# Feed-forward of a two-layer decoder: both parts of the tokens in one 512-column product, and the gate's K tiles ahead of the up's

## The reference

```
gate, up = split(h @ w_gu, (2816, 2816))
x = x + rms_norm((silu(gate) * up) @ w_down, g_post_ffn)      # the block

gate, up = split(conv3(h @ ffn_w_up) + conv_b, (2816, 2816))
x = x + (silu(gate) * up) @ ffn_w_down                        # layers 0 and 1
```

## Time and profile before

| What | Value |
|---|---|
| Time, median of 3 runs | 1380.72 us (1380.65 to 1381.92) |
| The profiled execution's own time | 1385.28 us |
| Its span in the trace | 1383.7 us |
| Mean granted TensorE clock | 0.98 |
| TensorE matmul busy | 1324.0 us, 96%, 8862 matmuls |
| DVE busy | 898.0 us, 65% |
| ACT busy | 685.7 us, 50% |
| POOL busy | 157.1 us, 11% |
| Read from HBM | 210.25 MB |

### The profile page before, as it was taken

How to read it: one execution, slowest core, us unless ns; L and a number is a source line. 1 busy time by engine, 2 the same in 40 slices (tenths; PEclk the granted TensorE clock), 3 DMA queues, 4 the chain that set the end, 5 groups by cost and what they waited for, 6 DMA issues and landing times.

```text
span 1383.7 us, 21580 instructions
## 1 busy us (share of the span) xinstructions
PE 1324.0 (96%) x8862; PEld 1190.6 (86%) x8862; DVE 898.0 (65%) x1325; ACT 685.7 (50%) x1007; POOL 157.1 (11%) x240
## 2 busy tenths in 40 slices
PE   6999999999999999999998999799999889899999
PEld 6987899878998898899997777699999767799998
DVE  5455378878646747644455676577776777676666
ACT  5345455635525546533344554554444675544443
POOL 8000030022000000300001131000000160000000
PEclk9999999999999999999999999999999999999999
DMA  8531355432645436566664622366666412366662
GB/s 279 189 121 63 124 177 177 147 108 92 227 154 183 181 95 197 153 183 184 186 188 130 213 92 82 86 183 183 183 183 202 162 32 77 91 185 186 187 186 95
DMA packets 207761, 212.69 MB, mean 154 GB/s; under 512 B 7473, under 2 KB 153859, under 8 KB 207664
## 3 DMA queue, kind: packets, MB, share of 16 engines
q1 hardware_dynamic: 204592, 206.25, 47.3%
q0 software_dynamic: 2480, 4.02, 0.8%
q10 hardware_dynamic: 592, 1.05, 0.2%
HBM read 210.25 MB, written 1.05 MB: 153 GB/s over the span
## 4 chain that ended last, share of the span: by engine, by line
PE 67%; DVE 6%; ACT 4%; issue 1%; POOL 0%; DVEq 0%; ACTq 0%
PE psum_a L515 8%; PE psum_a L516 8%; PE psum_a L517 8%; PE psum_b L515 8%; PE psum_b L517 8%; PE psum_b L516 8%; PE psum_c L516 4%; PE psum_c L515 4%; PE psum_c L517 4%; DVE w_lo L466 2%; ACT w_hi L456 1%; PE psum_c L2507 1%; PE psum_c L2477 1%; ACT junk_rows L683 1%; PE psum_c L2425 1%
## 5 line engine op out<-in xcount | busy, mean ns | idle before, releaser
L466 DVE TENSOR_TENSOR w_lo<-raw,w_hi 128x2048 fp32r<-128x2048 f32 (+4 forms) x221 | 423.0, 1947 | 72.7 <-ACT w_hi L456 71.7
L456 ACT ACTIVATE w_hi<-raw 128x2048 fp32r<-128x2048 f32 (+3 forms) x231 | 369.3, 1631 | 30.1 <-PE psum_b L517 16.3
L515 PE MATMUL psum_a<-x_hi,w_hi 128*128 128x256 f32 x752 | 216.2, 287 | 2.2 <-DVE w_lo L505 2.1
L515 PE MATMUL psum_b<-x_hi,w_hi 128*128 128x256 f32 x752 | 214.0, 285 | 0.8 <-issue 0.8
L516 PE MATMUL psum_a<-x_lo,w_hi 128*128 128x256 f32 x752 | 214.4, 285 | 0.0
L517 PE MATMUL psum_a<-x_hi,w_lo 128*128 128x256 f32 x752 | 214.2, 285 | 0.0
L516 PE MATMUL psum_b<-x_lo,w_hi 128*128 128x256 f32 x752 | 213.3, 284 | 0.0
L517 PE MATMUL psum_b<-x_hi,w_lo 128*128 128x256 f32 x752 | 213.2, 284 | 0.0
L515 PEld LDWEIGHTS psum_a<-x_hi,w_hi 128*128 128x128 f32 x752 | 146.1, 194 | 4.2 <-DVE w_lo L505 2.8
L516 PEld LDWEIGHTS psum_a<-x_lo,w_hi 128*128 128x128 f32 x752 | 146.0, 194 | 1.2
L515 PEld LDWEIGHTS psum_b<-x_hi,w_hi 128*128 128x128 f32 x752 | 144.8, 193 | 2.4 <-issue 0.9
(11 more groups left out here) (504 smaller groups left out, 2490.2 us busy)
## 6 DMA issues: line engine op xcount, KB each, us to landing
raw<-in_ffn_w_up_dram SPq DMA_DIRECT2D x88, 512.0 KB, 5.1
raw<-in_w_in_dram SPq DMA_DIRECT2D x40, 1024.0 KB, 5.6
raw<-in_w_gu_dram SPq DMA_DIRECT2D x44, 512.0 KB, 5.1
raw<-in_ffn_w_down_dram SPq DMA_DIRECT2D x44, 512.0 KB, 3.6
raw<-in_w_down_dram SPq DMA_DIRECT2D x22, 512.0 KB, 5.7
raw<-in_w_br_ssm_dram SPq DMA_DIRECT2D x8, 1024.0 KB, 5.0
raw<-in_w_xkv_dram SPq DMA_DIRECT2D x8, 1024.0 KB, 5.9
raw<-in_w_out_dram SPq DMA_DIRECT2D x8, 1024.0 KB, 5.1
```

Source lines behind the costliest of these rows:

```text
L456: act.activation(k.w_hi[:, s, 0:size], k.raw[:, s, 0:size], ACT.Copy).then_inc(*k.rounded.at(*key))
L466: dve.tensor_tensor(k.w_lo[:, s, 0:size], k.raw[:, s, 0:size], k.w_hi[:, s, 0:size].bitcast(F32), ALU.subtract).then_inc(*k.split.at(*key))
L515: pe.matmul(out_ap, l[0], r[0], start=start, stop=False, skip_group_check=True)
```

## The change

X becomes one tensor `X_both` of [128, 2 parts, 8 K tiles, 256 tokens]. `pe_gate_up` now issues, for each K tile and half, one matmul of w_hi with both parts of X (512 columns, in two chunks of 256) and one of w_lo with x_hi (256 columns). Each half has a bank of its own: columns 0 to 255 get w_hi x_hi and w_lo x_hi, columns 256 to 511 w_hi x_lo. Gate's eight K tiles come first, then up's; only block 0, which waits for X's K tiles one by one, keeps both halves inside the K loop. A signal `ffn_gate` tells that the gate's bank is made.

ACT copies the second half of each bank to SBUF (`both`), DVE adds the first half of the bank to it, and the taps, silu and product then read SBUF. Between them `dve_hidden` does the block's down piece in two halves (`dve_split_part`, the renamed `dve_split_third`), and DVE does the gate-and-up piece of h + 2 behind the hidden. `act_ffn` rounds two pieces ahead of every hidden but the first, so that its last one, behind the hidden of block 21, is now ahead of it. The memory keys are turned behind block 5's gate and up, into psum_a, and block 6 waits for their copy.

```diff
+        self.X_both = self.sb("x", [P, 2, KD, SEQ], F32R)
+        self.X = [self.X_both[:, part, :, :] for part in range(2)]
...
 def pe_gate_up(k, tag, h, after=None):
+    pe, ps, key = k.nc.tensor, ffn_ps(k, h), (tag, "gu", h)
     if h >= 2:
-        pe.wait_ge(*(k.ffn_h if tag == "ffn" else k.ffn_free).by(tag, h - 2))
-    for kt in range(KD):
-        if after:
+        pe.wait_ge(*k.ffn_both.by(tag, h - 2, 1))
+    for kt, j in [(kt, j) for kt in range(KD) for j in range(2)] if after else [(kt, j) for j in range(2) for kt in range(KD)]:
+        if after and j == 0:
             pe.wait_ge(*k.lo_made.by(after, kt))
-        for j in range(2):
-            mm = three(k, ps[:, j * SEQ:(j + 1) * SEQ], [x[:, kt, j * P:(j + 1) * P] for x in w], [x[:, kt, :] for x in k.X],
-                       kt == 0 and j == 0, kt == KD - 1)
+        hi, lo = (x[:, kt, j * P:(j + 1) * P] for x in w)
+        pe.matmul(ps[:, 512 * j:512 * j + 512].rearrange("p (n t) -> p n t", n=2), hi, k.X_both[:, :, kt, :], start=kt == 0,
+                  stop=False, skip_group_check=True)
+        mm = pe.matmul(ps[:, 512 * j:512 * j + SEQ], lo, k.X[0][:, kt, :], start=False, stop=kt == KD - 1, skip_group_check=True)
+        if (kt, j) == (KD - 1, 0):
+            mm.then_inc(*k.ffn_gate.at(tag, h))
...
 def act_hidden(k, tag, h, layer):
+    for j in range(2):
+        act.wait_ge(*(k.used.by(tag, "gu", h) if j else k.ffn_gate.by(tag, h)))
+        act.activation(k.both[:, u, j, :], ps[:, 512 * j + SEQ:512 * j + 512], ACT.Copy).then_inc(*k.ffn_copy.at(tag, h, j))
...
 def dve_hidden(k, tag, h, layer):
+    halves = h != FT - 3
+    for j in range(2):
+        dve.wait_ge(*k.ffn_copy.by(tag, h, j))
+        dve.tensor_tensor(k.both[:, u, j, :], ps[:, 512 * j:512 * j + SEQ], k.both[:, u, j, :], ALU.add).then_inc(*k.ffn_both.at(tag, h, j))
+    if halves:
+        dve_split_part(k, 0, 2)
...
+    if halves:
+        dve_split_part(k, 1, 2)
...
 def act_ffn(k, tag, layer):
     act_ffn_clear(k, tag)
-    act_split(k, 1)
-    act_hidden(k, tag, 0, layer)
-    for h in range(1, FT):
+    for h in range(FT):
...
-        act_split(k, 2 if h < FT - 1 else 1)
+        act_split(k, 2 if h else 1)
...
         act_hidden(k, tag, h, layer)
-    act_split(k, 1)
...
 def dve_ffn(k, tag, layer):
-    dve_split(k, 1)
-    dve_hidden(k, tag, 0, layer)
-    for h in range(1, FT):
+    inside = k.dve_split_at == k.place[tag, "gu", 1]
+    if inside:
+        dve_split(k, 1)
+    for h in range(FT):
...
-        dve_split(k, 2 if h < FT - 1 else 1)
         dve_hidden(k, tag, h, layer)
-    dve_split(k, 1)
+        if h < FT - 2:
+            dve_split(k, 1 if h != FT - 3 else 2)
+    if not inside:
+        dve_split(k, 1)
```

More of the change, by code:

```diff
@@ L394, in semaphores @@
              "o_hi", "o_lo"))
-        (self.ffn_clear, self.ffn_zero, self.ffn_pre, self.ffn_tap, self.ffn_silu, self.ffn_free, self.ffn_h, self.ffn_hi, self.ffn_lo) = (
-            new("ffn_" + n) for n in ("clear", "zeroed", "pre", "tap", "silu", "free", "h", "hi", "lo"))
+        (self.ffn_clear, self.ffn_zero, self.ffn_gate, self.ffn_copy, self.ffn_both, self.ffn_pre, self.ffn_tap, self.ffn_silu, self.ffn_h, self.ffn_hi,
+         self.ffn_lo) = (
+            new("ffn_" + n) for n in ("clear", "zeroed", "gate", "copy", "both", "pre", "tap", "silu", "h", "hi", "lo"))
         (self.head_copy_act, self.head_copy_dve, self.head_sq, self.head_sum, self.head_mean, self.head_root, self.fox_gate, self.fox_gate_act,
@@ L2092, in pe_ffn @@
 def pe_ffn(k, tag, norm):
+    pe = k.nc.tensor
     pe_gate_up(k, tag, 0, norm)
@@ L2095, in pe_ffn @@
     for h in range(1, FT):
-        if tag == "ffn" and h == 4:
+        if tag == "ffn" and h == 6:
+            pe.wait_ge(*k.k_mem_in.by())
+        pe_gate_up(k, tag, h)
+        if tag == "ffn" and h == 5:
+            pe.wait_ge(*k.ffn_both.by(tag, 4, 1))
             pe_memory_keys(k)
-        pe_gate_up(k, tag, h)
         if h < FT - 2:
@@ L2218, in pe_memory_keys @@
         for m in range(MT):
-            at = 512 + SEQ * j + P * m
-            mm = pe.transpose(k.psum_b[:, at:at + P], k.k_mem_rows[:, m, P * j:P * j + P], k.ident[:])
+            at = SEQ * j + P * m
+            mm = pe.transpose(k.psum_a[:, at:at + P], k.k_mem_rows[:, m, P * j:P * j + P], k.ident[:])
     mm.then_inc(*k.k_mem_turned.at())
@@ L2225, in act_memory_keys @@
     k.nc.scalar.wait_ge(*k.k_mem_turned.by())
-    k.nc.scalar.activation(k.k_mem_t[:, :, :], tiles_of(k.psum_b[:, 512:1024], 2), ACT.Copy).then_inc(*k.k_mem_in.at())
+    k.nc.scalar.activation(k.k_mem_t[:, :, :], tiles_of(k.psum_a[:, 0:512], 2), ACT.Copy).then_inc(*k.k_mem_in.at())
 def fox_rows(k, unit):
@@ L2729, in dve_fox @@
     dve_fox_turn(k, 3)
-    dve_split_third(k, 0)
+    dve_split_part(k, 0, 3)
     dve_fox_out(k, 2)
-    dve_split_third(k, 1)
-    dve_split_third(k, 2)
+    dve_split_part(k, 1, 3)
+    dve_split_part(k, 2, 3)
     dve_fox_peaks(k, 3)
     dve_fox_normalize(k, 3)
-    dve_split_third(k, 0)
-    dve_split_third(k, 1)
+    dve_split_part(k, 0, 3)
+    dve_split_part(k, 1, 3)
     dve_fox_turn_prob(k, 3)
```

96 lines of the change are left out of this document (47 added, 49 removed).

## The result

| | Before | Change |
|---|---|---|
| Median time, 4 runs each, same chip | 1381.05 us | 1371.82 us |
| Ratio to before | | 0.9931, 95% interval 0.9915 to 0.9947 |
| Profiled execution: time, span | 1385.28, 1383.7 us | 1372.6, 1370.9 us |

The account below looks back on a forecast made before the run. TensorE's matmul spacing was taken to bound the three feed-forwards. Terms of -14.1 (fewer matmuls) and +2.1, +0.5, -0.55 (ends) gave -12.0 us; against the median of 1380.72 that is 1368.7 us, range 1366 to 1377.5.

Parts of the forecast that it names:

- I take 0.2267 ... 1056 x 13.3 ns = 14.1 us go.: Gate-and-up products: a merged 512-column matmul takes 0.2267 us, so 1056 fewer matmuls save 13.3 ns each, 14.1 us.
- the dearer matmul: Rival, gate-and-up: the new matmul pays 20 ns (0.2333 us) as in the down product; 7.0 us go, 1375.7 us; chance 0.24.
- Chunks priced singly: Rival, gate-and-up: each 256-column chunk pays its own price, 0.240 us; TensorE gains nothing, 1382.8 us; no-gain chance 0.13.
- the strided read that stalls: Rival, gate-and-up: strided read of X stalls the stream, 0.2533 us, 1396.9 us; slower by stream or block, chance 0.06.
- Does more: Rival, gate-and-up: the 512-column matmul takes its columns alone, 0.2133 us; 26.1 us saved with the ends, 1354.6 us; chance 0.05.
- The block's work costs nothing: Each feed-forward block: the added 1.6 us of ACT copies and DVE adds cost nothing while TensorE's order covers them.
- gate work done early pays for the two added steps: Hidden's chain in a block: lo part ends 4.8 us after the second bank despite added copy and add, now 4.7.
- +2.1: End of the second feed-forward: late hidden stalls TensorE 1.25 us, first addition at T + 8.75 against T + 6.65: +2.1 us.
- +0.5: End of the first feed-forward: hidden just in time, but the split behind it delays the first gain product: +0.5 us.
- -0.55: End of the third feed-forward: last piece's split moved forward, a 1.25 us step returns to the normal 0.70: -0.55 us.
- I expect a span near 1371.7: Whole kernel: -12.0 us from the profiled execution's span of 1383.7 us gives a span near 1371.7.
- Other stages changing by more than a microsecond: Sign of a wrong forecast in the new profile: stages other than the feed-forwards change by more than a microsecond.

Follow-up runs that it names:

- e1_apart: The change with the 512-column matmul issued as two of 256 again, all else kept: 1380.39 us, ratio 0.9987 to the kernel before.
- e7_banks: The change with psum_c allocated ahead of psum_a and psum_b, so the down product writes the first four banks: 1372.24 us, ratio 0.9912 to the kernel before.
- e4_grouped: The change with each bank's eight 512-column matmuls first, then its eight of 256, except in block 0: 1369.77 us, ratio 0.9920 to the kernel before.
- e6_joined: The change with X's two parts side by side per K tile, so the 512 columns are one chunk: 1372.28 us, ratio 0.9922 to the kernel before.
- e8_double: The change with ACT's copy and DVE's add of every half-bank done twice, the extra into a spare tile: 1374.97 us, one run.
- e5_gate_late: The change with ACT waiting for both banks of a block before copying either: 1371.95 us, ratio 0.9917 to the kernel before.
- e2_tail: The change with ACT's last rounding of each feed-forward behind block 21's hidden again: 1370.97 us, ratio 0.9923 to the kernel before.
- e3_clear8: The change with eight clearing matmuls of psum_c instead of four in each feed-forward: 1377.02 us, one run.
- e10_stop: e2_tail with the down product's stop flag set only in the last block: 1369.56 us, one run.

## Why the prediction was right, and where its sizes were off

The forecast was 1368.7 us in 1366 to 1377.5, faster; it is 1371.82, faster. The mechanism is the one forecast: e1_apart takes the merging away and the gain goes with it.

- **"I take 0.2267 ... 1056 x 13.3 ns = 14.1 us go."** This is the term that was mis-sized: 9.2 ns a place, 9.2 us over the 63 products counted, so 9.7 us in all 66 blocks. About 1.5 of the 4.4 us too many are rounding: the text's own 5.74 us for 48 matmuls is 13.0 ns a matmul, not 13.3, and 5.74 to 5.55 us in 66 blocks is 12.6 us. The other 3 us are the slower half of the blocks, 33 x 0.09 us. The two reasons given for choosing the lower of two row prices were that the banks and the weights are those of rows that pay 13.3 ns. e7_banks shows that banks don't matter, in e4_grouped a 512 and a 256 with the same operands pay 18 and 12 ns, and the row chosen stands late in a run of 512s whose first six were at 0.232. Half of the blocks have the forecast pair of 0.347 us, the other half 0.3525, next to the dearer matmul's 0.3533, whose pace was named as a sign of a wrong forecast. The truth lies between forecast and that rival, a mixture that the text didn't allow for. With the measured terms the sum is -9.7 + 2.03 - 0.56 = -8.2 us, against -8.4 in the stages and -9.2 in the medians.
- **The prices not taken.** "Chunks priced singly" (0.240) and the strided read that stalls (0.2533) fall: e6_joined has no chunks and the same time. "Does more" (0.2133) falls too. e1_apart against the change shows 9.1 ns for each matmul saved, and not the 2.5 ns that the Trainium skill gives in TensorE: Matmul & The Clock Gate, section Part 1.
- **The block's work costs nothing.** Right, with the margins about as worked out: lo part 4.9 us after the bank (4.8 forecast), 3.3 us of margin (3.5), 3.7 for the split (3.7). e8_double adds the same work again without a gap in mid-stretch. The reason "gate work done early pays for the two added steps" is weak, by e5_gate_late: 0.35 us, and not needed.
- **Inside the chain two errors cancel.** The product ends 3.6 us after the bank (3.75 forecast), since the four taps take 1.66 us from SBUF and not 1.78. Then POOL's cast takes 0.80 us, which the working had vanish beside the half split, and the lo part waits for it (idle 0.29 in its row). In mid-stretch that is inside the margin; at the ends of the first two feed-forwards the same 0.29 stands in the chain that ends in the gain products and the additions.
- **The ends.** +2.1 was +1.85, with a stall of 1.33 for 1.25 and the lo part's end at T + 6.73 for 6.85. +0.5 was +0.18: the hidden of the first feed-forward was in time (743.91 + 0.43 = T + 5.27, forecast 5.35), and the gain product came 0.26 later instead of 0.5. -0.55 was -0.56. e2_tail takes the first two away and so shows their cause.
- **"I expect a span near 1371.7"** against 1370.9. That closeness is luck: the mis-sized term, 4.4 us too large, is made up by the 4.4 us of the attention stage. "Other stages changing by more than a microsecond" was named as a sign of a wrong forecast, and it came true there: the forecast had no term for the clock of a stage that the change leaves alone. The third feed-forward, -4.06, gave 0.3 us more than its terms, and that is the clock too: in both profiles of before the clock is at 1.2 GHz until 7.2 us into this stage, in the change until 6.5, and block 1 starts 12.27 us into it, in the change 11.83. e1_apart, with the matmuls of before and the clock of the change (until 6.7), has 12.02; e2_tail, with the matmuls of the change and the clock of before (until 7.3), 12.15.

## What to carry to other kernels

Where TensorE fills its stretch, read its price from start times as columns plus something per instruction, and count instructions: merging two moving operands that share weights into one matmul paid 9.2 ns each time here, against two added steps on engines with 3 us to spare. But a price read in one place isn't the price in another, even for one shape: with rows at 13.3 and 20 ns, take the middle and keep both, and look at what stands beside the matmul in each row. A piece of work moved ahead of a hidden that something waits for is free in mid-stretch; at the two ends the rounding cost 1.88 and 0.19 us: keep the last turn in the old order. And before a difference of two profiles is explained, compare the stages whose code is unchanged, with their clock.

## What was not expected of the hardware

- **One stream, two paces.** The same 32 matmuls take 5.55 or 5.64 us, alternating block by block. Which blocks get which changes within the first feed-forward, behind the memory keys of block 5, and differs in the second or third from kernel to kernel (reversed in e3_clear8, e6_joined, e7_banks, e8_double and e10_stop), also where TensorE's order is the same; what sets it is not shown. Grouped by shape there is one value, 5.60. The sums lie within 117.4 to 117.7 us in every kernel that has the merged matmul. What keeps them equal is not known.
- **A cast on POOL takes twice as long beside a DVE subtraction of two SBUF operands.** Groups of the whole kernel, first of before, then of the change:

```profile
L2089 POOL CAST ffn_hidden_hi<-ffn_h 128x256 fp32r<-128x256 f32 x66 | 26.5, 401 | 533.5 <-DVE ffn_h L2078 361.9
```

```profile
L2107 POOL CAST ffn_hidden_hi<-ffn_h 128x256 fp32r<-128x256 f32 x66 | 51.5, 780 | 501.3 <-DVE ffn_h L2094 341.1
```

  In the changed kernel block 19 is the one without half splits, and there DVE is idle during the cast; POOL's timeline has it beside its neighbour, block 20:

```profile
1052.06 0.40 POOL L2107 CAST ffn_hidden_hi<-ffn_h 128x256 fp32r<-128x256 f32 x1 [7.32 <-DVE ffn_h L2094]
1060.73 0.80 POOL L2107 CAST ffn_hidden_hi<-ffn_h 128x256 fp32r<-128x256 f32 x1 [8.27 <-DVE ffn_h L2094]
```

  The Trainium skill says of this in GPSIMD Engine Reference, section 1. Specifications, that POOL shares its SBUF interfaces with VectorE and that they contend when DVE reads two SBUF inputs; the trace agrees, 0.40 against 0.80 us. The half split beside it is shorter, 0.68 us, so that the lo part waits 0.29 us for the cast: nothing in mid-stretch, and 0.29 us at each of the first two ends.
